# Two transformer blocks on one core: six equal places for the expert weights of the second block, and scatter sums kept in PSUM

## What is computed

```python
def expert_choice_moe(x, w_router, b_router, w_gate, w_up, w_down):
    cap = CAPACITY_FACTOR * s // N_EXPERTS            # 2 * 256 // 16 = 32 tokens
    aff = jax.nn.softmax(x @ w_router + b_router, axis=-1)
    gate, idx = lax.top_k(aff.transpose(0, 2, 1), cap)
    xs = x[bidx, idx]
    hid = jax.nn.silu(xs @ w_gate) * (xs @ w_up)      # 16 experts, 1024 x 1024 each
    ys = (hid @ w_down) * gate[..., None]
    return jnp.zeros_like(x).at[bidx, idx].add(ys)

x = x + mixed @ w_out
x = x + expert_choice_moe(rms_norm(x, norm_ffn), w_router, b_router, w_gate, w_up, w_down)
```

## Time and profile before

| | |
|---|---|
| median of 3 runs | 1913.69 us |
| profiled execution, span | 1912.6 us |
| PE busy | 1630.2 us (85%) |
| DVE, ACT, POOL busy | 789.5, 313.7, 191.0 us |
| DMA | 599.81 MB, mean 314 GB/s |
| expert layers, first select to last load used | about 900 to 1333 us, and 1477 to 1909 us |

### The profile page before, as it was taken

How to read it: one execution, slowest core, us unless ns; L and a number is a source line. 1 busy time by engine, 2 the same in 40 slices (tenths; PEclk the granted TensorE clock), 3 DMA queues, 4 the chain that set the end, 5 groups by cost and what they waited for, 6 DMA issues and landing times.

```text
span 1912.6 us, 25365 instructions
## 1 busy us (share of the span) xinstructions
PE 1630.2 (85%) x10752; PEld 936.6 (49%) x10752; DVE 789.5 (41%) x1528; ACT 313.7 (16%) x825; POOL 191.0 (10%) x177
## 2 busy tenths in 40 slices
PE   8999999999999999999775766758999885756757
PEld 3455999444579964474332232322574432232322
DVE  1586788877738886666010100102576010010101
ACT  1243111021511101362000000001253000010000
POOL 0011034000214410320000000000220000000000
PEclk9999999999999999999997887979999897887978
DMA  9992998434365643647999999999846999999998
GB/s 357 338 353 90 331 338 281 154 132 176 118 200 179 242 147 122 203 176 296 417 430 428 429 432 424 433 429 408 263 178 267 414 431 432 424 432 426 432 428 354
DMA packets 165960, 599.81 MB, mean 314 GB/s; under 512 B 20976, under 2 KB 79856, under 8 KB 142064
## 3 DMA queue, kind: packets, MB, share of 16 engines
q1 hardware_dynamic: 165630, 598.04, 79.9%
q10 hardware_dynamic: 242, 0.53, 0.1%
HBM read 594.76 MB, written 3.80 MB: 313 GB/s over the span
## 4 chain that ended last, share of the span: by engine, by line
PE 54%; DMA 38%; DVE 4%; ACT 2%; issue 1%; SPq 0%; POOL 0%; DVEq 0%; ACTq 0%; POOLq 0%
DMA extra<-in_w_down 14%; DMA extra<-in_w_up 13%; DMA extra<-in_w_gate 11%; PE ps L1421 7%; PE ps L1448 7%; PE ps L1786 5%; PE ps L1375 5%; PE ps L1046 4%; PE ps L1215 4%; PE ps L1492 4%; PE ps L1317 3%; PE ps L1664 3%; PE ps L1523 3%; PE ps L1806 1%; DMA ring<-in_w_mod 1%
## 5 line engine op out<-in xcount | busy, mean ns | idle before, releaser
L1786 PE MATMUL ps<-ring,wide 128*32 128x256 f32 x2912 | 217.1, 463 | 124.3 <-DMA ring<-in_w_up 76.4
L1786 PEld LDWEIGHTS ps<-ring,wide 128*32 128x32 f32 x2912 | 107.1, 132 | 227.5 <-DMA ring<-in_w_up 85.6
L3536 DVE TENSOR_TENSOR wide<-ps,wide 128x512 f32<-128x512 f32 x16 | 10.7, 670 | 502.8 <-PE ps L1786 502.8
L1806 PE MATMUL ps<-ring,wide 128*32 128x512 f32 x768 | 157.5, 638 | 46.7 <-DMA ring<-in_w_down 46.6
L1786 PE MATMUL ps<-extra,wide 128*32 128x256 f32 x1056 | 89.5, 510 | 59.1 <-DMA extra<-in_w_up 35.5
L1806 PEld LDWEIGHTS ps<-ring,wide 128*32 128x32 f32 x768 | 42.0, 117 | 158.1 <-issue 124.3
L1421 PE MATMUL ps<-hT,ring 128*128 128x128 f32 x960 | 114.7, 276 | 0.0
L1421 PEld LDWEIGHTS ps<-hT,ring 128*128 128x128 f32 x960 | 111.0, 192 | 1.0 <-issue 1.0
L1375 PE MATMUL ps<-hT,ring 128*128 128x128 f32 (+1 forms) x704 | 100.2, 304 | 0.0
L2356 ACT ACTIVATE wide<-ps 128x512 f32<-128x512 f32 x8 | 4.8, 597 | 564.4 <-PE ps L1806 422.2
L1375 PEld LDWEIGHTS ps<-hT,ring 128*128 128x128 f32 x704 | 94.0, 192 | 5.7 <-issue 1.0
(11 more groups left out here) (408 smaller groups left out, 2413.4 us busy)
## 6 DMA issues: line engine op xcount, KB each, us to landing
ring<-in_w_gate SPq DMA_DIRECT2D x24, 4096.0 KB, 31.6
ring<-in_w_down SPq DMA_DIRECT2D x24, 4096.0 KB, 33.5
ring<-in_w_up SPq DMA_DIRECT2D x20, 4096.0 KB, 32.4
ring<-in_w_mod SPq DMA_DIRECT2D x24, 2048.0 KB, 13.0
ring<-in_w_up SPq DMA_DIRECT2D x44, 1024.0 KB, 10.1
extra<-in_w_gate SPq DMA_DIRECT2D x8, 4096.0 KB, 35.1
extra<-in_w_up SPq DMA_DIRECT2D x8, 4096.0 KB, 33.4
ring<-in_w_in SPq DMA_DIRECT2D x13, 2048.0 KB, 9.9
```

The lines of the kernel that those rows point to most:

```text
L1786: last = mm(ps[2 * part + e // 2][j * CAP:(j + 1) * CAP, e % 2 * 2 * P:(e % 2 + 1) * 2 * P], xsT[:, k, e * CAP:(e + 1) * CAP], expert_row( ...
L1806: last = mm(ps[6 + n][e * CAP:(e + 1) * CAP, :], hidT[:, e, k, :], expert_row(n0, e, k)[:, n * N:(n + 1) * N], start=k == 0, stop=k == KD - 1)
```

## The change

- **Six places of 4 MB.** Units take six places in a fixed turn: ring slots 2-3, ring slots 4-5, `far_pair`, ring slots 0-1, `near_pair`, `edge_pair`. The whole of unit 4 (near) and unit 5 (edge) is loaded before unit 0 is used. Near and edge are used by every sixth unit of the layer from then on. `once_part`, `early_part` and `row_part` go.
- **The order of loads.** Three quarters of the edge pair are issued right after the bias loads and before the output tiles. The fourth is issued with pair 2. The near pair comes in four pieces: 0 after mixed_sumsq (as before), 3 after pair 3 and ffn_sumsq, 1 after the router product, 2 after ffn_normed. Then unit 6 comes in two halves, each as a half of unit 0 has been used. Unit 0 itself is loaded in two halves by rows.
- **x is given up.** near_pair lies over a part of wide, hT, all of x and most of spare. x is rebuilt at the last group by two ScalarE activations from xk times the reciprocal of rff (`moe_restored`), once unit 46 has been used.
- **Scatter in PSUM.** The scatter products of all four groups add up in banks 4 to 7 and are added to x once a layer. The other products of a group move to banks 0 to 3.
- **Space.** Tiles are joined into `near` and `far`, small scratch of the routing moves to the end of spare, and dynamic_dma_scratch_size is set to 1,024 bytes. The first group is written out ahead of the loop in the PE, ACT and DVE programs.

```diff
-G_SLOTS = SLOTS + PAIR
+G_SLOTS = SLOTS + 3 * PAIR
+FAR_SLOT, NEAR_SLOT, EDGE_SLOT = SLOTS, SLOTS + 1, SLOTS + 2
+PAIR_SLOTS = (2, 4, FAR_SLOT, 0, NEAR_SLOT, EDGE_SLOT)
...
+        near = sb("near", [P, 6144 + 2048 + NC_ * D + 2816])
+        wide, hT = near[:, 0:6144], near[:, 6144:8192]
+        x = near[:, 8192:8192 + NC_ * D].rearrange("p (c d) -> p c d", c=NC_)
+        near_pair = near[:, 4096:4096 + UNIT_SIZE]
...
+        edge_pair, far_pair = far[:, live:live + UNIT_SIZE], extra[:, PIECE:PIECE + UNIT_SIZE]
...
         def pair_slot(n):
-            return SLOTS + 1 if n == G_PAIRS else (2, 4, SLOTS, 0)[(n if n < G_PAIRS else n - 1) % G_PAIRS]
+            return PAIR_SLOTS[n % G_PAIRS]
...
+                for e in range(EG - 1):
+                    piece(edge_unit, e)
                 for t in range(SLOTS, B2_HEAD):
                     head_tile(t)
-                early_part()
 
                 sp.wait_ge(tile_done, b2_used(L, 3))
-                pair(0)
+                first_pair()
                 sp.wait_ge(tile_done, b2_used(L, 5))
                 sp.wait_ge(*s.at("b2_taps_ready", 1))
                 pair(1)
                 sp.wait_ge(*s.at("att_values_done", MAPS2))
                 pair(2)
-                once_part(0)
+                piece(edge_unit, EG - 1)
                 sp.wait_ge(*s.at("b2_out_flipped", 5))
                 sp.wait_ge(*s.at("b2_mixed_sumsq", 2))
-                once_part(1)
+                piece(near_unit, 0)
                 sp.wait_ge(tile_done, b2_used(L, 7))
                 pair(3)
+                sp.wait_ge(*s.at("b2_ffn_sumsq", 4))
+                piece(near_unit, 3)
                 sp.wait_ge(*s.at("b2_router_done", 2))
-                once_part(2)
-                sp.wait_ge(*s.at("b2_slots_flipped", 2))
-                once_part(3)
+                piece(near_unit, 1)
+                sp.wait_ge(*s.at("b2_ffn_normed", 2))
+                piece(near_unit, 2)
                 for i in range(PAIR):
                     sp.wait_ge(tile_done, g_used(L, 0, i))
-                    row_part(i)
-                for n in range(G_PAIRS + 2, GROUPS * G_TILES // PAIR):
-                    sp.wait_ge(tile_done, g_used(L, 0, PAIR * pair_before(n) + PAIR - 1))
+                    half_pair(G_PAIRS, i)
+                for n in range(G_PAIRS + 1, GROUPS * G_TILES // PAIR):
+                    sp.wait_ge(tile_done, g_used(L, 0, PAIR * (n - G_PAIRS) + PAIR - 1))
...
-                def scatter(s, c, n):
-                    mm(ps[4 - 2 * c + n][:, :], pgT[:, c, :], ysb[:, n * N:(n + 1) * N], start=True, stop=True)\
-                        .then_inc(s.up("g_scatter_done"), 1)
+                def scatter(g, c, n):
+                    at_ = g if isinstance(g, int) else 1
+                    return mm(ps[4 + 2 * c + n][:, :], pgT[:, c, :], ysb[:, n * N:(n + 1) * N], start=at_ == 0, stop=at_ == GROUPS - 1)
...
+                    ends = isinstance(g, int) and g == GROUPS - 1
+                    if ends:
+                        moe = Count(sems, L, COUNTS, None)
+                        act.wait_ge(tile_done, g_used(L, g, G_TILES - PAIR - 1))
+                        act.wait_ge(*moe.at("moe_inverse", 1))
+                        for c in range(2):
+                            av(x[:, c, :].rearrange("p (q k) -> p q k", k=KD), xk[:, c, :, :].rearrange("p k q -> p q k"),
+                               ACT.Copy, scale=rffi[:, c:c + 1]).then_inc(moe.up("moe_restored"), 1)
```

More of the change, by code:

```diff
@@ L404, in two_blocks @@
         ysb = wide[:, 3072:4096]
[L405 to L411, removed]
+        selP = spare[:, 2048:2304].rearrange("p (c e s) -> p c e s", c=2, e=EG)
+        selG = spare[:, 2304:2560].rearrange("p (c e s) -> p c e s", c=2, e=EG)
+        pgT = spare[:, 2560:2816].rearrange("p (c t) -> p c t", c=2)
+        rscratch, rsel, rcum = spare[:, 2048:2304], spare[:, 2304:2560], spare[:, 2560:2816]
         gfin = qk[:, 0:D]
@@ L419, in two_blocks @@
         tile_done = sems.pop("tile_done")
-        arrived = [ctx.enter_context(nc.semaphore(f"slot_loaded{i}")) for i in range(SLOTS + 2)]
+        arrived = [ctx.enter_context(nc.semaphore(f"slot_loaded{i}")) for i in range(SLOTS + 3)]
         def b1_slot(t):
@@ L817, in head_tile @@
                     else:
-                        sp.wait_ge(tile_done, g_used(L - 1, 0, GROUPS * G_TILES - 1 - PAIR * (3 - t // 2)))
+                        last = max(n for n in range(LAST_UNIT + 1) if pair_slot(n) == t // PAIR * PAIR)
+                        sp.wait_ge(tile_done, g_used(L - 1, 0, PAIR * last + PAIR - 1))
                     dst = slot2(t)
@@ L849, in pair, with first_pair, piece, half_pair @@
                                  pair_rows(n).rearrange("p e k n -> p e (k n)")).then_inc(arrived[pair_slot(n)], 16)
[L851 to L862, removed]
+                def first_pair():
+                    for k in range(PAIR):
+                        sp.dma_start(pair_at(0).rearrange("p (k e m) -> p k e m", e=EG, k=PAIR)[:, k, :, :], pair_rows(0)[:, :, k, :])\
+                            .then_inc(arrived[pair_slot(0)], 16)
+                def piece(n, e):
+                    sp.dma_start(pair_at(n)[:, e * PIECE:(e + 1) * PIECE], pair_rows(n)[:, e, :, :].rearrange("p k n -> p (k n)"))\
+                        .then_inc(arrived[pair_slot(n)], 16)
+                def half_pair(n, i):
+                    half = UNIT_SIZE // PAIR
+                    sp.dma_start(pair_at(n)[:, i * half:(i + 1) * half], pair_rows(n)[:, i, :, :].rearrange("p k n -> p (k n)"))\
+                        .then_inc(arrived[pair_slot(n)], 16)
                 for t in range(SLOTS):
@@ L1829, in group_head @@
                     select(range(1, 2)).then_inc(s.up("g_rows_done"), 1)
[L1830 removed]
+                    if isinstance(g, int) and g == 0:
                         pe.wait_ge(*s.at("g_rows_by_dve", 1))
@@ L1863, in group_tail @@
                     for i in range(4):
-                        scatter(s, i // 2, i % 2)
+                        scatter(g, i // 2, i % 2)
                     s.end()
@@ L3531, in group @@
                     rows_evac(3)
+                    moe = Count(sems, L, COUNTS, None)
+                    if isinstance(g, int) and g == 0:
+                        nc.vector.reciprocal(rffi, rff).then_inc(moe.up("moe_inverse"), 1)
                     dve.wait_ge(*s.at("g_gate_silu", 2))
@@ L3539, in group, with add @@
                                             hv.rearrange("p (e c k) -> p e k c", e=2, k=KD)).then_inc(s.up("g_hidden_flipped"), 1)
-                    def add(i, c, n):
-                        dve.wait_ge(*s.at("g_scatter_done", i + 1))
+                    def add(i):
+                        c, n = i % 2, i // 2
+                        dve.wait_ge(*moe.at("moe_restored", c + 1))
+                        dve.wait_ge(*moe.at("moe_scattered", i + 1))
                         xv = x[:, c, n * N:(n + 1) * N]
-                        tt(xv, ps[4 - 2 * c + n][:, :], xv, ALU.add).then_inc(s.up("g_scatter_added"), 1)
-                    if isinstance(g, int):
-                        add(0, 0, 0)
+                        tt(xv, ps[4 + 2 * c + n][:, :], xv, ALU.add).then_inc(moe.up("moe_added"), 1)
+                    ends = isinstance(g, int) and g == GROUPS - 1
+                    if ends:
+                        add(0)
                     dve.wait_ge(tile_done, g_used(L, g, G_TILES - 1))
-                    cp(ysb[:, N:2 * N], ps[7][:, :]).then_inc(s.up("g_result_by_dve"), 1)
-                    if isinstance(g, int):
+                    cp(ysb[:, N:2 * N], ps[1][:, :]).then_inc(s.up("g_result_by_dve"), 1)
+                    if ends:
                         for i in range(1, 4):
-                            add(i, i % 2, i // 2)
-                    else:
-                        for i in range(4):
-                            add(i, i // 2, i % 2)
+                            add(i)
                     s.end()
-                with dve.Fori(0, GROUPS - 1) as g:
+                group(0)
+                with dve.Fori(1, GROUPS - 1) as g:
                     group(g)
```

98 lines of the change are left out of this document (53 added, 45 removed).

## The result

The changed kernel took 1902.34 us (median of 4 runs, 1901.22 to 1904.92) against 1914.39 us for the kernel before (4 runs): 12.05 us less, a ratio of 0.9936 with a 95% interval of 0.9922 to 0.9951. Forecast were 13.8 us less, 1899.9 us, with a range of 1897 to 1904.5; the narrower range of the forecast proper, 1897.5 to 1902, is missed by 0.3 us. The profiled execution's span fell from 1912.6 to 1900.2 us.

A forecast was written before the change was run, and what follows sets the result against it. The prediction took the unbroken DMA stream to bound the expert layers, with PE the chain in the layers' first part. Bytes 4.90 and holes 2.0 us a layer, twice, made 13.8 us: 1913.7 to 1899.9 us, range 1897 to 1904.5.

The forecast's parts named there:

- rival A: Holes at the stream's start stay or move because a piece comes late; only the bytes gained, 1903.9 us; chance 0.13.
- What bounds the kernel: Expert layers end at stream start plus remaining bytes at 9.80 us a unit, plus holes, plus a tail.
- Where the stream begins: In each expert layer the unbroken DMA stream begins with pair 3, at 887.58 us, not with the first expert product.
- half a unit instead of three quarters: Ahead of pair 3, 4.25 units come instead of 3.75; half a unit gains 4.90 us a layer.
- The holes: Two DMA pauses early in each layer's stream, over 903 to 906 and 912 to 915 us, vanish: 2.0 us a layer.
- The piece rule of the Trainium skill: About 2 us per transfer would give back 2 us of 6.9 a layer; the forecast counted queued pieces' bytes only.
- Steady state: Within the unbroken stream, more units on their way, held SP, later waits and PE's shorter path between groups: no effect.
- the written-out first group: The group written out ahead of the loop was to cost nothing, within 1 us either way.
- The tail: At the layer's end, two activations rebuilding x stay hidden with 1.4 us to spare: 0, at worst 2.5 us late.
- B: The rebuild of x at the layers' end comes late, losing 2 x 2.5 us: 1904.9 us; chance 0.06.
- C: Fuller queue or new places slow both layers' streams; 0.16 us a unit decides against the change; 1920 us; chance 0.05.
- D: Something else sets the stream's end: layer start slips or longer programs cost the gain; about 1912 us; chance 0.06.

The follow-up runs named there:

- e7: The changed kernel with two of the four edge pieces (half a unit) issued after the last near piece, in the stream; 1912.69 us, ratio 0.9986.
- e8: The changed kernel with both halves of unit 6 waiting until unit 1 is used, not for the halves of unit 0; 1914.53 us, ratio 0.9997.
- e15: The changed kernel, but from unit 12 a load waits for the unit four before it, not six; 1904.08 us, ratio 0.9938.
- e5: The changed kernel with the second group's PE program back in the loop and zero products opening the scatter banks; 1901.26 us, ratio 0.9926.
- e1: The changed kernel run once more, nothing altered; 1903.9 us, ratio 0.9938 of the kernel before.
- e13: The changed kernel again, on the same chip as e14; 1902.59 us, ratio 0.9933 of the kernel before.
- e14: The kernel of e5 once more, on the same chip as e13; 1899.77 us, ratio 0.992 of the kernel before.

## Why the prediction was right, point by point

The mechanism was right, and 12.05 of the 13.8 us came. That the median lies in the range is in part luck: 1902.34 us is above the 1902 of the forecast's own range, and the stretch up to 1904.5 was there for rival A, which did not occur. What took the difference was another term, named below.

- **What bounds the kernel: right.** Stream start, bytes, holes and tail account for the difference, and e7 and e8 moved the end by the bytes and the pause put in.
- **Where the stream begins, and half a unit instead of three quarters: right.** 4.90 us a layer; e7 measured 5.35 and 4.65 for the same half against the changed kernel's first trace, and up to unit 7, before most of the loads, 4.99 and 4.60.
- **The holes: right in place and cause.** With the bytes, 6.9 us a layer were forecast; up to unit 7 it was 6.98 and 6.22, and by the mean of unit 7's 16 parts 6.91 and 6.82. The last near piece was issued at 894.71 us, 9 us before the one ahead of it had landed (903.76). e8 shows a hole put back at its full width.
- **The piece rule of the Trainium skill ("SBUF — State Buffer", "The DMA setup-cost knee"): didn't show.** With one piece more in the stream nothing of the 2 us a piece appeared before unit 7. The two more pieces of e7 cost 4.99 and 4.60 us up to unit 7, and their bytes alone are 4.90. The row that I had taken it from, 890 to 903 us in rows 5, was thinner ground than I made of it: it holds little of the second piece, which was issued at 899.12 us and landed at 905.40.
- **Steady state "cost and gain nothing": wrong in one term.** The held SP, the later waits and the shorter path between groups did cost nothing (e15, e5). But the stream itself became 1.03 and 1.86 us longer. The step that failed is "the written-out first group: nothing, within 1 us either way": I looked at the path of the engines for it and not at the DMA engines, where its code travels. It measured 1.1 us in the mean of the parts over both layers (0.55 us each), 2.7 and 1.1 us in the streams of two pairs of executions (e1 and e5, e13 and e14), and 2.8 us between medians on one chip. Without it the time fell by 13.6 us (e5) and 15.8 us (e14), and e5's streams by 14.4 us, so that the forecast's 13.8 us are met by one kernel of the two and passed by the other.
- **The tail: right.** Rebuilding x was hidden with 1.1 and 1.2 us to spare where I had 1.4; the end after the last landing took 7.42 instead of 7.33 us.
- **The rivals.** A and B didn't occur. C's sign was there, 0.03 to 0.05 us a unit of the 0.16 that would have turned the result, but by another cause than queue or places. D named longer programs and had the size wrong.

## What to carry to other kernels

In a stretch bound by DMA, find the moment from which the queue never runs empty, and count the bytes that are still to come then; a buffer more is worth only what it moves ahead of that moment. Then look for each instant at which the next load waits for an engine while the queue drains: PE at full work says nothing about it. And keep code out of such a stretch: a loop body instead of a written-out copy saved 1.1 to 2.8 us here, by streams or by medians, and the engines' work on the experts was the same.

## What the runs showed of the hardware that I had not expected

- Instruction loads of 16 KB travel through the same 16 DMA engines as the weights, one packet each, for 0.88 to 1.51 us. Each one delayed the mean of a unit's 16 parts by 0.09 us over 24 streams. Five or six more a layer made the stream 1.0 and 1.9 us longer by its last part in one execution, 0.7 and 0.4 us in another of the same kernel.
- A unit lands with its slowest part. In the unbroken stream the 16 parts drifted apart, to 4.4 us in the first layer and 5.9 us in the second, and did not come together again before the stream's end; in the last 3 us about half of the DMA engines' time was empty.
- An issue can hold SP for 10 to 20 us when much is queued (20.10 us for one part of the last unit). In the groups, where e15 removes these holds, they cost nothing.
- Transfers of 1 MB queued behind others land 2.5 us apart (unit 4's pieces at 901.28, 903.76 and 906.25 us), the time of their bytes at 423 GB/s.
